# Prompt stick-breaking attention: the causal mask added in PSUM by matmuls, logits in two halves, outputs by head pair

## The reference, cut to what matters

```
def block(args):                       # blocks of 128 queries
    mask = k_pos[None, :] < q_pos[:, None]
    z = einsum('bqhd,bkhd->bhqk', qb, k) * scale + bias
    log_keep = where(mask, log_sigmoid(-z), 0.0)
    later = cumsum(log_keep, axis=3, reverse=True) - log_keep
    a = where(mask, exp(log_sigmoid(z) + later), 0.0)
    return einsum('bhqk,bkhd->bqhd', a, v)
```

## Time and profile before

| | us |
|---|---|
| median of 3 runs | 2802.5 (2801.15 to 2815.39) |
| profiled execution, its own time | 2800.47 |
| its span | 2798.7 |
| TensorE busy | 2661.9 |
| VectorE busy | 1197.7 |
| ScalarE busy | 810.7 |
| GpSimd busy | 93.5 |

### The profile page before, as it was taken

The page is one execution under the profiler, slowest core; times in us unless marked ns, Lnnn a source line. Parts: engine busy times, 40 slices in busy tenths (PEclk is TensorE's granted clock), DMA queues, the critical chain, the costliest instruction groups (busy, mean ns, idle before and its releaser), DMA issues.

```text
span 2798.7 us, 44375 instructions
## 1 busy us (share of the span) xinstructions
PE 2661.9 (95%) x18965; PEld 2524.1 (90%) x18965; DVE 1197.7 (43%) x1545; ACT 810.7 (29%) x990; POOL 93.5 (3%) x178
## 2 busy tenths in 40 slices
PE   6999999999887999999999999999978799999999
PEld 6999999999555799999999999999954589999998
DVE  6343335671444243334453443345237414433343
ACT  5222224442123232212333222224235323222221
POOL 1000000000112000000000000001010110000000
PEclk8999999999988899999999999999888869999999
DMA  5323322122222123232224223223210222223322
GB/s 175 87 67 86 87 73 76 57 84 68 55 88 65 46 76 86 72 90 83 66 85 126 75 72 93 76 72 118 79 67 5 77 73 76 75 79 86 90 59 81
DMA packets 334522, 220.72 MB, mean 79 GB/s; under 512 B 11849, under 2 KB 326497, under 8 KB 334420
## 3 DMA queue, kind: packets, MB, share of 16 engines
q1 hardware_dynamic: 325268, 185.83, 23.0%
q0 software_dynamic: 9152, 33.43, 3.7%
HBM read 206.78 MB, written 12.45 MB: 78 GB/s over the span
## 4 chain that ended last, share of the span: by engine, by line
PE 91%; DVE 6%; ACT 2%; issue 1%; DMA 0%; SPq 0%; DVEq 0%; ACTq 0%
PE psum L506 70%; PE psum L528 6%; PE psum L2201 1%; PE psum L2222 1%; PE psum L1416 1%; PE psum L1475 1%; PE psum L1467 1%; PE psum L2051 1%; PE psum L1726 1%; DVE rest L2124 1%; PE psum L2223 1%; PE psum L2040 1%; PE psum L1606 1%; PE psum L1456 1%; PE psum L1616 1%
## 5 line engine op out<-in xcount | busy, mean ns | idle before, releaser
L506 PE MATMUL psum<-act_hi,whi 128*128 128x288 f32 (+2 forms) x3504 | 753.4, 297 | 11.7 <-DVE act_lo L759 4.6
L506 PE MATMUL psum<-act_hi,wlo 128*128 128x288 f32 (+2 forms) x3504 | 752.3, 296 | 0.0
L506 PE MATMUL psum<-act_lo,whi 128*128 128x288 f32 (+2 forms) x3504 | 752.2, 296 | 0.0
L506 PEld LDWEIGHTS psum<-act_hi,whi 128*128 128x128 f32 (+2 forms) x3504 | 562.3, 187 | 13.5 <-issue 4.2
L506 PEld LDWEIGHTS psum<-act_hi,wlo 128*128 128x128 f32 (+2 forms) x3504 | 562.6, 187 | 0.4
L506 PEld LDWEIGHTS psum<-act_lo,whi 128*128 128x128 f32 (+2 forms) x3504 | 562.2, 187 | 0.3
L485 DVE TENSOR_TENSOR wlo<-raw,whi 128x2048 fp32r<-128x2048 f32 x190 | 435.4, 2292 | 233.3 <-ACT whi L478 233.2
L478 ACT ACTIVATE whi<-raw 128x2048 fp32r<-128x2048 f32 x190 | 362.0, 1905 | 301.7 <-PE psum L506 297.8
L506 PE MATMUL psum<-h_hi,whi 128*128 128x288 f32 x1408 | 302.0, 295 | 0.0
L506 PE MATMUL psum<-h_hi,wlo 128*128 128x288 f32 x1408 | 301.9, 295 | 0.0
L506 PE MATMUL psum<-h_lo,whi 128*128 128x288 f32 x1408 | 301.9, 295 | 0.0
(11 more groups left out here) (387 smaller groups left out, 2280.3 us busy)
## 6 DMA issues: line engine op xcount, KB each, us to landing
raw<-in_w_ffn_up SPq DMA_DIRECT2D x176, 512.0 KB, 4.9
raw<-in_w_ffn_down SPq DMA_DIRECT2D x64, 384.0 KB, 3.9
raw<-in_w_ffn_down SPq DMA_DIRECT2D x64, 320.0 KB, 3.5
raw<-in_w_out SPq DMA_DIRECT2D x16, 512.0 KB, 4.3
raw<-in_w_in_a SPq DMA_DIRECT2D x14, 512.0 KB, 4.6
raw<-in_w_in_a SPq DMA_DIRECT2D x16, 384.0 KB, 3.9
raw<-in_w_kv SPq DMA_DIRECT2D x12, 512.0 KB, 4.4
vpg<-in_cache_v POOLq DMA_DIRECT2D x16, 384.0 KB, 3.5
```

The costliest lines, as they stand in the source:

```text
L506: last = pe.matmul(psum[0:width, 4 * j + 2 * m + h, 0:HALF], w[:, k, cols], a[:, k, h * HALF:(h + 1) * HALF], start=(k == 0 and step == 0) ...
```

## The change

It does four things in the prompt attention, and one at setup.

1. The masks of VectorE go. At setup GpSimd makes one 128 x 128 tile that is 0 below the diagonal and -1e30 elsewhere, and ScalarE copies it and the identity to fp32r (`mask_r`, `ident_r`). Behind the logits of each tile a matmul of the identity with the mask adds it to the diagonal block in PSUM.
2. The logits of a head stand in whole banks: tile 3 in bank 0, tile 2 in bank 1, tiles 1 and 0 in bank 2. Tile 3 with its mask is released first, the other three with theirs second. ScalarE reads 512 columns, then 768, in two operations each, and gives each half free by itself.
3. VectorE scans tile 3 first, behind the first half's release, and the others behind the second's.
4. The transposed weights have two buffers, `a_t` for even heads and `work` (the memory of `tmp` and `sqt`) for odd ones. TensorE issues the outputs of a pair once both are there, r = 0 and r = 1 in turn, and the lo of pair p stands behind head 2p + 3 on VectorE instead of 2p + 5.

```
+        work = sb("work", [P, 4 * TOK])
+        mask_f = tmp[0][:, 0:P]
+            select(mask_f[:, :], ALU.is_ge, NEG, -1, [[-1, P]], 1)
+            act.activation(ident_r[:, :], ident[:, :], ACT.Copy)
+            act.activation(mask_r[:, :], mask_f[:, :], ACT.Copy)
-        Z_AT = (896, 1024, 512, 0)
+        Z_PSUM = (1280, 1024, 512, 0)
+        Z_AT = (1152, 896, 512, 0)
+            def z_mask(t):
+                at = Z_PSUM[t] + t * P
+                return pe.matmul(flat[:, at:at + P], ident_r[:, :], mask_r[:, :], start=False, stop=True, skip_group_check=True)
             def z(h):
                 if h:
-                    pe.wait_ge(S.z_read, h)
-                for t in range(4):
-                    last = pe.matmul(flat[:, Z_AT[t]:Z_AT[t] + (t + 1) * P], qb_t[r, h // 2, t * P:(t + 1) * P],
-                                     kt_b[r, h // 2, 0:(t + 1) * P], start=True, stop=True)
+                    pe.wait_ge(S.z_read, 2 * h - 1)
+                z_tile(h, 3)
+                z_mask(3).then_inc(S.z_ready, 1)
+                if h:
+                    pe.wait_ge(S.z_read, 2 * h)
+                for t in (2, 1, 0):
+                    z_tile(h, t)
+                for t in (2, 1, 0):
+                    last = z_mask(t)
                 last.then_inc(S.z_ready, 1)
-            def outputs(h):
-                pe.wait_ge(S.at_ready, h + 1)
+            def outputs(p):
+                pe.wait_ge(S.at_ready, 2 * p + 2)
-                if h >= 4 and h % 2 == 0:
-                    pe.wait_ge(S.stick_lo, h // 2 - 1)
+                if p >= 2:
+                    pe.wait_ge(S.stick_lo, p - 1)
                 for k in range(4):
+                    for r in range(2):
+                        h = 2 * p + r
...
             for h in range(HB):
                 if h + 1 < HB:
                     z(h + 1)
-                if h:
-                    outputs(h - 1)
+                if h and h % 2 == 0:
+                    outputs(h // 2 - 1)
                 pe.wait_ge(S.a_ready, h + 1)
+                if h:
+                    pe.wait_ge(S.at_ready, h)
...
+                act.activation(tk[:, 0:Z_HALF], flat[:, 0:Z_HALF], ACT.Sigmoid, scale=scale, bias=b)
+                act.activation(kp[:, 0:Z_HALF], flat[:, 0:Z_HALF], ACT.Sigmoid, scale=-scale, bias=neg).then_inc(S.z_read, 1)
+                act.wait_ge(S.z_ready, 2 * h + 2)
+                act.activation(z_late(tk), z_late_psum(), ACT.Sigmoid, scale=scale, bias=b)
+                act.activation(z_late(kp), z_late_psum(), ACT.Sigmoid, scale=-scale, bias=neg).then_inc(S.z_read, 1)
+                if h >= 3 and h % 2 == 1:
+                    stick_hi(act, h // 2 - 1)
...
-                for x, m, op in ((tk, before, ALU.mult), (kp, not_before, ALU.max)):
-                    for at in (384, 768, 1152, 896):
-                        ins = dve.tensor_tensor(x[:, at:at + P], x[:, at:at + P], m[:, :], op)
-                step(ins)
-                for t in range(4):
+                for t in (3, 2, 1, 0):
+                    if t >= 2:
+                        dve.wait_ge(S.z_read, 2 * h + 4 - t)
...
-                if h % 2 == 1 and h > 4:
-                    stick_lo(dve, h // 2 - 2)
+                if h >= 3 and h % 2 == 1:
+                    stick_lo(dve, h // 2 - 1)
```

More of the change, by code:

```diff
@@ L294, in build @@
         rinv = sb("rinv", [P, TOK])
-        tmp = [sb(f"tmp{j}", [P, TOK]) for j in range(2)]
-        sqt = [sb(f"sqt{j}", [P, TOK]) for j in range(2)]
+        work = sb("work", [P, 4 * TOK])
+        tmp = [work[:, j * TOK:(j + 1) * TOK] for j in range(2)]
+        sqt = [work[:, (2 + j) * TOK:(3 + j) * TOK] for j in range(2)]
+        mask_f = tmp[0][:, 0:P]
         mk_t = [sb(f"mk_t{l}", [P, 2, M]) for l in range(2)]
@@ L318, in build @@
         w_pad = sb("w_pad", [NSA, P])
-        before = sb("before", [P, P])
-        not_before = sb("not_before", [P, P])
+        ident_r = sb("ident_r", [P, P], F32R)
+        mask_r = sb("mask_r", [P, P], F32R)
         own_keys = sb("own_keys", [96, 2, NS])
@@ L568, in setup_pool @@
             pool.memset(ones_heads[:, :], 0.0)
-            for t, v in ((ident, 0.0), (causal, 0.0), (causal_b, 0.0), (own, 1.0), (before, 1.0), (not_before, 0.0), (rep, 0.0)):
+            for t, v in ((ident, 0.0), (causal, 0.0), (causal_b, 0.0), (own, 1.0), (mask_f, 0.0), (rep, 0.0)):
                 pool.memset(t[:, :], v)
@@ L2021, in inb_dve, with z_late, z_late_psum, z_tile @@
             dve.wait_ge(S.region_free1, BASE_OUTB // 2)
-        Z_AT = (896, 1024, 512, 0)
+        Z_PSUM = (1280, 1024, 512, 0)
+        Z_AT = (1152, 896, 512, 0)
+        Z_HALF = 512
         A_AT = (0, 512, 1024, 896)
         ZW = 1280
+        a_turn = (a_t, work)
+        def z_late(t):
+            return t[:, 512:1280].rearrange("p (b n) -> p b n", b=2)
+        def z_late_psum():
+            return psum[:, 1:3, 0:384]
         def stick_pe(pe):
             pe.wait_ge(S.ma_out_lo, 10)
+            def z_tile(h, t):
+                r = slice(64 * (h % 2), 64 * (h % 2) + 64)
+                pe.matmul(flat[:, Z_PSUM[t]:Z_PSUM[t] + (t + 1) * P], qb_t[r, h // 2, t * P:(t + 1) * P],
+                          kt_b[r, h // 2, 0:(t + 1) * P], start=(t > 0), stop=False, skip_group_check=True)
+            def z_mask(t):
+                at = Z_PSUM[t] + t * P
+                return pe.matmul(flat[:, at:at + P], ident_r[:, :], mask_r[:, :], start=False, stop=True, skip_group_check=True)
@@ L2050, in outputs @@
                 for k in range(4):
-                    last = pe.matmul(psum[64 * (h % 2):64 * (h % 2) + 64, 6 + (h // 2) % 2, k * P:NPR], vp[:, k, h * DB:(h + 1) * DB],
-                                     a_t[:, A_AT[k]:A_AT[k] + NPR - k * P], start=(k == 0), stop=(k == 3), skip_group_check=True)
+                    for r in range(2):
+                        h = 2 * p + r
+                        last = pe.matmul(psum[64 * r:64 * r + 64, 6 + p % 2, k * P:NPR], vp[:, k, h * DB:(h + 1) * DB],
+                                         a_turn[r][:, A_AT[k]:A_AT[k] + NPR - k * P], start=(k == 0), stop=(k == 3),
+                                         skip_group_check=True)
@@ L2066, in stick_pe @@
                 last.then_inc(S.a_turned, 1)
-            outputs(HB - 1)
+            outputs(HB // 2 - 1)
         def stick_act(act):
```

28 lines of the change are left out of this document (10 added, 18 removed).

## The result

| | us |
|---|---|
| changed kernel, median of 4 runs | 2776.72 (2773.58 to 2778.70) |
| kernel before, median of 4 runs | 2803.43 (2801.15 to 2815.39) |
| ratio | 0.9895, 95% interval 0.9865 to 0.9925 |
| span of the profiled execution | 2774.2, before 2798.7 |

The changed kernel is about 1% faster, 27 us by the medians. When it was run again beside the kernel before, twice, its ratio was 0.9899 (0.9873 to 0.9925) and 0.9913 (0.9887 to 0.9938). So the effect is there each time, and one such comparison gives its size to about 0.3 of itself.

A forecast was written before the change was run, and what follows sets the result against it. It took TensorE and VectorE to take turns in the prompt attention. TensorE's work 67.9 + low clock 9.5 + end waits 3.3 = 80.7 us against 112.06; 2800.47 - 31.4 + 0.3 setup = 2769.4, predicted 2769, range 2758 to 2784.

The forecast's parts named there:

- TensorE becomes the bound, a pair in 11.3 us: Prompt attention: a head pair costs TensorE 11.3 us, VectorE 10.0, ScalarE 8.8; the pair was 17.8.
- VectorE's head 4.63, its 20.9 us count only as far as TensorE can follow: Masks off VectorE: a head falls from 6.37 to 4.63 us, 20.9 us in all, counting only as TensorE follows.
- Mask matmuls 0.13, shape changes 0.1: TensorE's masks: 0.52 us a head, plus 0.2 for changes of array shape; z with masks 3.07.
- Outputs of a pair 2.7: TensorE's outputs issued in turn: column halves overlap, 2.7 us a pair instead of 4.6, ends 2.3 and 4.6.
- Transposes 1.24: TensorE's transposes in the prompt attention: 1.24 us a head at full clock, 14.9 in the sum.
- No lo wait and no gap that lowers the clock: TensorE's outputs: the 17.8 us wait for lo has no successor, nor has the gap that lowered the clock.
- 20 us at the low level at the start, ends 10 and 24.4: Start of the stage: 20 us at the low clock lose 9.5 us; ends 10 us (4.7 lost) and 24.4 (11.6).
- 3.3 us of waits at the end: End of the stage: TensorE waits about 2.0 us for head 11's weights and 1.3 for its copy.
- Two halves on ScalarE: ScalarE: two more operations a head add 0.3 us busy; take starts after tile 3 instead of all of z.
- rival E: ScalarE and TensorE: half-by-half waits make a ring, some 1.5 us a head, 18 us, total 2787; chance 0.05.
- Rival B: TensorE's outputs: the halves don't overlap, 11.4 us more, total 2780.5; chance 0.14.
- Rival D: TensorE's clock stays low through the stage, 132 us with the end, total 2820; chance 0.03.

The follow-up runs named there:

- e9: Kernel before, with hi and lo earlier and masks added by four TensorE matmuls a head, one release of logits: 2791.13 us, ratio 0.9944.
- e3: Kernel before, with one edit of order, hi and lo of pair p at head 2p + 3: 2789.69 us, ratio 0.9931.
- e8: Changed kernel run again with no edit: 2773.61 us, ratio 0.9899 to the kernel before.
- e5: Changed kernel with a head's logits released once and both halves' buffers freed once: 2801.35 us, ratio 0.998 to the kernel before.
- e1: Changed kernel with a pair's eight output matmuls issued head by head instead of in turn: 2783.78 us, ratio 0.9923 to the kernel before.
- e6: Changed kernel with dense matmuls, 8 ahead of the first z, 4 behind z(0), 8 behind z(1), 4 behind z(2): 2785.67 us, ratio 0.9917.
- e4: Changed kernel with ten dense matmuls ahead of the first z: 2780.63 us, ratio 0.9908 to the kernel before.
- e7: Changed kernel with ten dense matmuls behind z(1): 2776.05 us, ratio 0.9898 to the kernel before.

## Why the prediction was right, and where its sum was off

The direction, the place and the bound were right: 2769 was forecast, 2776.7 measured, inside 2758 to 2784. The stage was forecast at 80.7 us and took 86.3 in the profiled execution, 77.4 and 86.1 in two others. That the sum came as near as it did is in part luck: its 20 us of low level lie between lengths that the trace before gave no means to foresee, and errors in other terms nearly cancel. By the steps:

- *TensorE becomes the bound, a pair in 11.3 us.* Right: 11.23, all of it TensorE's in the chain.
- *VectorE's head 4.63, its 20.9 us count only as far as TensorE can follow.* Right, and e9 sharpens it: with the outputs head by head TensorE takes 12.96 a pair, so that of VectorE's saving of 3.5 a pair only 0.3 shows.
- *Mask matmuls 0.13, shape changes 0.1.* z with masks was taken as 3.07, measured 3.28, 2.5 us more in the sum. Four masks in a row are 0.59 (e9), 0.15 each. The two groups cost the rest, 0.34 a head, where the prediction had 0.20 for the shape changes. The Trainium skill's sentence on the drain (TensorEngine Tiling (Array Packing), Key Properties) pointed the right way; by the rows a second group costs 0.34 us, and no run here shows whether that is a drain.
- *Outputs of a pair 2.7.* Measured 2.31 in the chain, which is full overlap, 2.3 us less in the sum. The estimate by the Trainium skill's span model (TensorE: Matmul & The Clock Gate, Measured speedup vs the span model) was 2.3; the trace agrees, with both streams starting at 2133.78.
- *Transposes 1.24.* Right behind outputs; behind masks they took 1.11 or 1.12, 0.7 us less in the sum.
- *No lo wait and no gap that lowers the clock.* Right: no such row among the waits, and 1.00 from 2124.93 to 2177.99. e3 shows that this step alone is 17.2 of the 25.8 us, or over half at equal low levels.
- *20 us at the low level at the start, ends 10 and 24.4.* **This is the term that was mis-sized.** It was 33.2 us in the profiled execution, outside the ends, and costs 0.474 x 13.2 = 6.3 us more. In e8 it was 14.3. The step took a length from one execution of another kernel and argued that a closed gap would shorten it; the runs show that the length is no property of the kernel. It also took the first z for the start of the low level, which in the kernel before had begun 9.9 us earlier.
- *3.3 us of waits at the end.* Measured 1.91 for head 11's weights and 1.33 for its copy, 3.2.
- With the measured terms the sum is 12 x 3.28 + 6 x (1.24 + 1.12) + 6 x 2.31 = 67.4, + 0.474 x 33.2 = 15.7, + 3.2: 86.3, measured 86.28. For e8, with 14.3, the same sum gives 77.4, measured 77.4.
- *Two halves on ScalarE.* The prediction counted them as 0.3 us of ScalarE's time and an earlier start, and did not see what they carry: without them the changed order is at 0.998 (e5). The forecast held only because the halves were there. Its rival E described this ring, and argued that no resource is loaded enough for it. Load was the wrong test; what matters is what stands between one z and the next in TensorE's order.
- *Rival B, 11.4 us for outputs that don't overlap.* They overlap. The price without the alternation is 9 us (e1), since one matmul in four of the second head overlaps anyway.
- *Rival D* needed 87 us at the low level. The longest seen at the start was 36.5, in e5. What was said for it, that transposes do not count for the clock, no run here bears out: in e6, e8 and e1 the level rose during the first ten transposes or right behind them.

What stays open is what ends the low level at the start. Bursts of dense work (e4, e6, e7) did not decide it, and two executions of one kernel differ by 19 us. Nor is it shown why the stage's start moves between runs.

## What to carry to other kernels

Before a cost is taken off the busiest-looking engine, look in the chain for what is queued behind what: here a hi that stood one head later than it had to, and a lo that stood two, cost more than all the masks. When work is gathered into larger pieces (the outputs of two heads), ask what it stood in front of, since it may have been the cover of a buffer's release; a release in two halves can stand in for a second buffer. Matmuls with 64 stationary columns for two halves of the array should be issued in turn: here, in fp32, 2.30 us for eight instead of 3.86. And a stage that starts at the low clock should be profiled more than once before a difference of some microseconds is explained.

## What the runs showed of the hardware that I had not expected

- Two streams of fp32 matmuls with 64 stationary columns each overlap completely when they alternate: 2.30 us for twice the work of 2.30 us. Issued one stream after the other, they still overlap by one matmul, 3.86 us (e1).
- With the granted clock at 0.50, TensorE can be fully busy for 28.75 us and keep that level, while in e8 z, masks and transposes, with the outputs of pairs among them, hold 1.00 for 49 us.
- The low level at the start lasted 14.3, 33.0 and 33.2 us in three executions of one kernel. That is 9 us of time, a third of what the change gains. The six executions of e8 spread over 21 us, 0.8%; the fastest had a mean granted clock of 0.959 over the whole span and the slowest 0.953. So single executions of this kernel cannot be compared below 1%.
- A mask matmul of 128 columns costs 0.15 us in a row of four (e9), and z in two groups with masks between them 0.34 us more than in one.
